# Hybrid decoder layer: where the sample tokens' q/k/v projection is issued among the attention tiles

## What is computed

```
xn = rmsnorm(x)                                 # all 1088 tokens
[a, b, q, k, v, g_A, g_B] = xn @ w_in
q, k = rmsnorm per head of 64; 16 q heads in 4 groups, 4 k/v heads
s = q.k / 8 + bias(distance), masked to a window of 128, with a learned sink per head
o = softmax([s, sink])[:-1] @ v                 # prompt: blocks of 128 queries against 256 keys
```

## Time and profile before

| | us |
|---|---|
| median of 3 launches | 1377.56 (1376.6 to 1383.25) |
| the profiled launch | 1377.99 |
| its span, first to last instruction | 1375.4 |
| PE busy in the span | 1251.6 (91%) |
| DVE busy | 1079.2 (78%) |
| ACT busy | 706.2 (51%) |
| POOL busy | 275.8 (20%) |
| tile 6 on PE, `turn_qk` to `turn_qk` | 236.5 to 265.8 |
| tile 7 and the end of the attention phase | 265.8 to 305 |

### The profile page before, as it was taken

One profiled execution on the slowest core, in us unless ns is written; L12 is line 12 of the kernel. 1 busy time (PEld: TensorE's weight loads), 2 busy tenths in 40 slices (PEclk: granted clock), 3 DMA queues, 4 the chain that ended last, 5 costly groups with the idle time before them and its releaser, 6 DMA issues. The chain is left out here.

```text
span 1375.4 us, 23543 instructions
## 1 busy us (share of the span) xinstructions
PE 1251.6 (91%) x8743; PEld 742.0 (54%) x8743; DVE 1079.2 (78%) x1299; ACT 706.2 (51%) x1160; POOL 275.8 (20%) x279
## 2 busy tenths in 40 slices
PE   5899999859999999999999999989949999888885
PEld 2456666646666666666656666645524555444442
DVE  5788887865869999999994976536577999778773
ACT  4656656545233442344233654324116888676773
POOL 1281111100000110011000000000342567324322
PEclk9999999959799999999999999999968999999998
DMA  8700000201214443344321055374887999899962
GB/s 324 159 10 1 0 0 0 104 21 64 57 39 125 103 102 80 83 117 116 83 64 60 32 191 191 112 301 163 301 295 229 327 319 368 327 333 324 335 238 42
DMA packets 53070, 211.18 MB, mean 154 GB/s; under 512 B 14560, under 2 KB 15776, under 8 KB 40416
## 3 DMA queue, kind: packets, MB, share of 16 engines
q1 hardware_dynamic: 31888, 156.94, 31.4%
q0 software_dynamic: 18672, 44.42, 13.7%
q10 hardware_dynamic: 2448, 8.98, 1.6%
HBM read 180.97 MB, written 39.72 MB: 160 GB/s over the span
## 5 line engine op out<-in xcount | busy, mean ns | idle before, releaser
L1294 DVE SCALAR_TENSOR_TENSOR big<-c_region,c_taps,big 128x1024 f32<-128x1024 f32 (+1 forms) x120 | 153.7, 1281 | 3.7 <-ACT caT L994 3.7
L72 PE MATMUL c_psb<-xnT,w_taken 128*128 128x364 f16 x456 | 146.5, 321 | 2.4 <-DVE f_w_l L1189 2.4
L73 PE MATMUL c_psb<-xnT,w_taken 128*128 128x364 f16 x456 | 146.5, 321 | 0.0
L74 PE MATMUL c_psb<-xnT,f_w_l 128*128 128x364 f16 x456 | 146.3, 321 | 0.0
L1294 DVE SCALAR_TENSOR_TENSOR caT<-c_region,c_taps,caT 128x1024 f32<-128x1024 f32 x112 | 143.4, 1280 | 0.0
L72 PE MATMUL o_psH<-e_gu,big 128*128 128x512 f16 x256 | 100.6, 393 | 4.1 <-DVE big L2284 2.5
L73 PE MATMUL o_psH<-e_gu,big 128*128 128x512 f16 x256 | 101.0, 395 | 0.0
L74 PE MATMUL o_psH<-e_gu,big 128*128 128x512 f16 x256 | 100.6, 393 | 0.0
L72 PE MATMUL c_psa<-xnT,w_taken 128*128 128x364 f16 x312 | 99.1, 318 | 0.0
L74 PE MATMUL c_psa<-xnT,f_w_l 128*128 128x364 f16 x312 | 99.0, 317 | 0.0
L73 PE MATMUL c_psa<-xnT,w_taken 128*128 128x364 f16 x312 | 99.0, 317 | 0.0
(11 more groups left out here) (378 smaller groups left out, 3432.3 us busy)
## 6 DMA issues: line engine op xcount, KB each, us to landing
e_gu<-w_gu SPq DMA_DIRECT2D x34, 1024.0 KB, 24.1
w_taken<-w_feat SPq DMA_DIRECT2D x48, 512.0 KB, 4.1
e_d<-w_dn SPq DMA_DIRECT2D x17, 1024.0 KB, 22.9
xnT<-w_gu SPq DMA_DIRECT2D x14, 1024.0 KB, 31.2
big<-w_gu SPq DMA_DIRECT2D x14, 1024.0 KB, 32.3
c_region<-gates POOLq DMA_DIRECT2D x8, 1092.0 KB, 5.8
xnT<-w_dn SPq DMA_DIRECT2D x7, 1024.0 KB, 30.1
big<-w_dn SPq DMA_DIRECT2D x7, 1024.0 KB, 30.1
```

What stands on the lines that cost most here:

```text
L72: pe.matmul(out, stat[0], mov[0], start=start, stop=False)
L73: pe.matmul(out, stat[0], mov[1], start=False, stop=False)
L74: return pe.matmul(out, stat[1], mov[0], start=False, stop=stop)
L1294: dve.scalar_tensor_tensor(y_j, glu[:, p, j:j + SEQ], tap, y_j, op0=ALU.mult, op1=ALU.add).then_inc(tap_done, 1)
```

## The change

The six half pieces of the sample tokens' projection are split over tiles 6 and 7. PE's tile 6 (`pieces=2`) issues the first four where they were. The last two (columns 1024 to 1535) leave tile 6 and go to tile 7 (`pieces=1`), one behind `scores` 1, one behind `turn_p` 0. ACT's copy of that piece and the squares of the sample tile follow it into tile 7, behind `exps` 1. DVE's `mean_squares(8)` moves from the head of tile 7 to the place directly ahead of `norms(8)`. PE's loop is one turn shorter, with tiles 5, 6 and 7 written out; ACT writes out tiles 6 and 7, DVE tile 7. No work is added or dropped.

```diff
 ACT
-            def tile(t, first=False, last=False):
+            def tile(t, first=False, pieces=3):
...
                 turned_p(t, 0, first)
                 exps(t, 1, lo)
+                if pieces == 1:
+                    piece(t + 1, 2)
+                    squares(t + 1)
                 turned_p(t, 1, first)
...
-                if not last:
+                if pieces > 2:
                     piece(t + 2, 2)
                     squares(t + 2)
...
-            with act.Fori(1, NT - 1) as t:
+            with act.Fori(1, NT - 2) as t:
                 tile(t)
-            tile(NT - 1, last=True)
+            tile(NT - 2, pieces=2)
+            tile(NT - 1, pieces=1)
 DVE
                 split_qkv(t)
-                mean_squares(t + 1)
+                if not last:
+                    mean_squares(t + 1)
                 logits(t, 0, lo)
...
                 low_p(2)
+                if last:
+                    mean_squares(t + 1)
                 norms(t + 1)
                 output(t, 2)
...
-            with dve.Fori(1, NT) as t:
+            with dve.Fori(1, NT - 1) as t:
                 tile(t, False)
+            tile(NT - 1, False, True)
 PE
                 scores(t, odd, 1, first)
-                if not last:
+                if pieces > 1:
                     half_piece(t + 2, 0, 1)
+                else:
+                    half_piece(t + 1, 2, 0)
                 scores(t, odd, 2, first)
                 turn_p(t, 0, first)
-                if not last:
+                if pieces > 1:
                     half_piece(t + 2, 1, 0)
+                else:
+                    half_piece(t + 1, 2, 1)
                 values(t, 0, first)
...
                 values(t, 1, first)
-                if not last:
+                if pieces > 2:
                     half_piece(t + 2, 2, 0)
                 turn_p(t, 3, first)
                 values(t, 2, first)
-                if not last:
+                if pieces > 2:
                     half_piece(t + 2, 2, 1)
                 values(t, 3, first)
...
-            with pe.Fori(0, NT // 2 - 1) as u:
+            with pe.Fori(0, NT // 2 - 2) as u:
                 tile(2 * u + 1, 1)
                 tile(2 * u + 2, 0)
-            tile(NT - 1, 1, last=True)
+            tile(NT - 3, 1)
+            tile(NT - 2, 0, pieces=2)
+            tile(NT - 1, 1, pieces=1)
```

More of the change, by code:

```diff
@@ L549, in _, with tile @@
             dve.memset(g.oT_l[:, :, T:TP], 0.0).then_inc(setup_done, 1)
-            def tile(t, first):
+            def tile(t, first, last=False):
                 lo = P if first else 0
@@ L695, in values, with tile @@
                 last.then_inc(o_done, 1)
-            def tile(t, odd, first=False, last=False):
+            def tile(t, odd, first=False, pieces=3):
                 turn_qk(t)
-                if not last:
+                if pieces > 1:
                     half_piece(t + 2, 0, 0)
```

## The result

The changed kernel takes 1383.99 us in the median of 20 launches, the kernel before, timed with it, 1377.57; the ratio is 1.0042 with a 95% interval of 1.0031 to 1.0054, that is 5.8 us slower (4.3 to 7.4). A second set of launches gave 1.0032 (1.0017 to 1.0046). The forecast was 4.35 us more, 1381.9 us.

The account below looks back on a forecast made before the run. Tile 6 was taken as paced by DVE, tile 7 by a ring of DVE, ACT and PE. A 5.10 us added wait less 0.75 gave +4.35 us, 1381.9 us against the 1377.56 median; range 1377.3 to 1386.0.

Parts of the forecast that it names:

- Two halves out of tile 6: End of tile 6: 5.2 us of PE work removed, gaining nothing at turn_p 3 and 0.22 us at values 3.
- The seam: Between tiles 6 and 7: q's high part starts 0.7 us later; bounds, gain 0.75 and loss 1.1 us.
- Means off the head of tile 7: Start of DVE's tile 7: removing mean_squares(8) frees nothing, since logits 0 waits for PE's scores.
- The halves fit into tile 7: PE around turn_p 0 of tile 7: both halves fit idle gaps, and turn_p 0 at full clock gains 0.87 us.
- Half pieces in the way: Rival, tile 7: first half at half clock makes turn_p 0 about 3 us late; +7.4 us, 1384.9; chance 0.09.
- Low part 2 over 0.75 us earlier: DVE in tile 7: low part 2 and what follows come 0.75 us earlier, with turn_p 2 at half clock.
- full-clock walk: Rival, tile 7: PE stays fast from the seam, low part 2 2.9 us earlier; +2.2 us, 1379.8; chance 0.22.
- The chain: End of DVE's tile 7: means, root and norms in succession start output 2 7.75 us after low part 2, adding 5.10.
- The loads: SyncE's loads move from 265.32 to about 282, land at about 294.5, 10 us before the barrier, and cost nothing.
- Carried through to the end: After the attention phase's barrier: later phases depend on it only, so the shift reaches the end unchanged.
- The sum: Whole launch: 5.10 - 0.75 = +4.35 us, 1381.9 us against the median; chance of the forecast 0.53.
- The clock downstream: Rival, convolution: the shift keeps PE fast there, up to 8.5 us off; -4.2 us, 1373.4; chance 0.06.

Follow-up runs that it names:

- e5: The changed kernel unedited, launched again on one chip beside the kernel with norms(8) last; ratio to the kernel before 1.0032 (1.0017 to 1.0046).
- e2: Changed kernel with DVE's norms(8) of tile 7 moved behind output 3; ratio to the kernel before 0.9973 (0.9958 to 0.9989).
- e6: Changed kernel with norms(8) behind output 3, launched again on the changed kernel's chip; ratio to the kernel before 0.9984 (0.9969 to 0.9999).
- e1: Kernel before with only DVE's mean_squares(8) moved directly ahead of norms(8) in tile 7; ratio to the kernel before 1.0048 (1.0026 to 1.0070).
- e9: Changed kernel, norms(8) in its place, with empty matmuls in PE's idle stretches of tiles 6 and 7; ratio to the kernel before 0.9992 (0.9980 to 1.0004).
- e10: Changed kernel with norms(8) last and empty PE matmuls in tiles 6 and 7 and on into the convolution; ratio to the kernel before 0.9940 (0.9924 to 0.9956).

## Why the prediction was right, and where it was loose

- **Two halves out of tile 6 free nothing at `turn_p` 3, and 0.22 us at `values` 3.** Right. `turn_p` 3 started 4.26 us after `turn_p` 2 against 4.17, now behind an idle of 2.52 us for the exponentials. In e5, at full clock, `values` 3 came 8.15 us after the mark against 8.37 before; in the first profile it came 1.0 us later than before, behind a `turn_p` 3 at half clock.
- **The seam: a loss of 0.7 us, between a gain of 0.75 and a loss of 1.1.** Both ends occurred. DVE's first instruction of tile 7 came 12.85 us after the mark in the first profile and 11.12 in e5, against 11.84: 1.01 later and 0.72 earlier. The forecast named one value for what is a spread from launch to launch. Its reason for the value, that half clock came after every long gap in tile 7, was a wrong reading: `turn_p` 3 of tile 7 in the kernel before (293.60, shown above) follows an idle of 2.11 us and took 1.07 us.
- **Means off the head of tile 7 free nothing.** Right: DVE then waited 2.51 us for the scores (1.86 in e5). In the first profile the scores came later as well, behind a `turn_o` of 1.97 us instead of 1.30, and low part 0 started 1.0 us later than before, where 0.1 us earlier was expected (in e5 1.4 us earlier).
- **The halves fit into tile 7.** Right: the transposes between them took 1.06 us and waited 0.84 us for ACT, not for the half (PE rows above). "Half pieces in the way" did not happen.
- **Low part 2 over 0.75 us earlier (2.9 on the full-clock walk).** It was 0.0 in the first profile (36.61 against 36.60 us after the mark) and 3.1 in e5 (33.51); e2 and e6, the same up to this point, give 3.7 and 2.8. No profile shows the 0.75 that went into the sum. Three of four show the full-clock walk, which stood among the rivals with a chance of 0.22.
- **The chain: 7.75 us from low part 2 to output 2, 5.10 more than before.** Measured 7.73 in both profiles, in e1 and in e9. This term carries the result, and e1 and e2 show it by putting it in alone and taking it out alone.
- **The loads.** Right: they were issued at 283.23 instead of 265.32 and the last, issued at 285.05, took 10.9 us, so 296, 15 us ahead of the barrier.
- **Carried through to the end.** Between the marks the changed kernel lost 5.07 and 1.97 us, in time 5.8 and 4.4. Behind the barrier its two profiles have 1072.4 and 1074.4 us where the others have 1068.8 to 1072.3. So the changed kernel's profiles are 2.9 and 4.9 us longer there than the kernel before, a part that the forecast had at nothing. 1.70 us of it, in both, are the half-clock sums behind the convolution's taps (DVE waits 2.48 us for them instead of 0.78). Nobody edited that place; e6 and e10 have the same 1.70 us, and e9, which keeps the changed kernel's order of work, has not (1069.3 in all). This speaks for a clock that falls or holds there from launch to launch. Whether the changed kernel meets it more often stays open with two profiles.
- **The sum, and the luck in it.** The forecast was 4.35 us, and 5.8 (4.3 to 7.4) and 4.4 (2.3 to 6.3) were measured. The chain of 5.10 us was right and is no luck. The 0.75 us set against it are between two walks, and with the walk that three of four profiles took the forecast would have been 2.2 us. e5 did lose only 1.97 us between the marks; its span is 5.9 us longer than that of the kernel before because 4.9 us more were lost behind the barrier. That the time came out so close is thus partly luck.
- **The clock downstream.** It gave nothing to this change. Where it was forced (e10), PE gained 2.3 us at the head of the convolution and lost 1.70 of them at the next place where the clock fell.

## What to carry to other kernels

Moving work to an engine's idle stretch also moves everything that depends on it: list each consumer that stands in a strictly ordered queue (here DVE's norms), and see whether the short chain to it (here reduce, a root of 3.5 us on another engine, scale) still has cover. If not, move the consumer behind the steps that others wait for; here moving one call turned a loss of 4 to 6 us into a gain of 2 to 4, though that gain itself is mostly PE's clock in tile 7. And before taking PE's work away from a full stage, price what the idle time does to its clock: empty matmuls in the idle time of a single tile were worth 5 us.

## What the runs showed of the hardware that I had not expected

In the same program PE falls to half clock at different places from launch to launch: `turn_p` 3 of tile 6 took 1.94 us in one profile of the changed kernel and 1.07 in the other, and the stretch up to the barrier differed by 3.1 us. The sums behind the convolution's taps did the same, 400 us behind the edit: a pair of matmuls took 1.02 to 1.10 us in nine profiles and up to 1.92 in four, which cost 1.70 us each time. A single profile is therefore one walk of several, and marks at a step ahead of the edit were needed to compare them. Half clock in tile 7, where PE is waited for only in short turns between DVE and ACT, cost 5.2 us: 3.4 up to low part 2, about the idle time in front of DVE, and most of the rest in the last steps behind it.
